# A unit of the rest's merge spread over three batches, and the gather ring grown at gather 460 in place of 450

## The chip, the cores and the metric

The kernel runs on one NeuronCore of a Trainium2 chip. The metric is the device time of one execution in microseconds (us), lower is better. A program is timed several times, and the median is compared.

## What is computed

The reference is one layer of a decoder for 512 prompt rows and 8 x 8 sample rows (576 rows in all, 1024 features, float32): an mLSTM branch and three groups of dilated window attention, merged by sigmoid gates, and after that a retrieval of experts. Only the last two parts matter here:

```python
merged = jax.nn.sigmoid(parts[14]) * branch_a + jax.nn.sigmoid(parts[15]) * branch_b
x = x + ga1 * _rmsnorm(merged @ prm['w_out'], prm['g_post1'])
h2 = _rmsnorm(x, prm['g_pre2']) * (1 + sc2) + sh2
# _peer: 8 heads, 16 experts of 16384 per row and head, chosen by two sets of 128 keys
act = gelu(jnp.einsum('td,thkd->thk', hb, u[eidx]))
out = jnp.einsum('thk,thkd->td', g * act, v[eidx])
```

`parts[14]`, `parts[15]` and the branches are products of the normalised input and of the branch outputs with weights. Each row takes 8 x 16 experts, and each expert is a row of 1024 numbers of `u` and 1024 of `v`, side by side in one table `uv` (8 KB a row).

## The kernel before, in words

**Tiles.** The 576 rows are four tiles of 128 (0 to 3) and one of 64 (tile 4, the samples, which takes two heads at once in its two halves). Everything up to the merge of tiles 0 and 1 ends before the stretch that matters; `output_and_experts` is that stretch. It starts the experts of tiles 0 and 1 as soon as these have been merged, and does the merge of the other 320 rows ("the rest") beside them.

**Blocks and batches.** A block `b` is a tile and a head: 16 blocks for tiles 0 and 1, 16 for tiles 2 and 3, 4 for tile 4, 36 in all. A block gathers 16 experts per row, so there are 576 gathers `n`, each of 128 table rows (1 MB). Two gathers are a batch `g` (8 to a block, `q` is the batch's place in its block, `g = 8 b + q`). What each engine does for a batch: GpSimd issues its two indirect DMAs (L1705) into a slot of `ring`; VectorE takes the dot product of the `u` half with the row's input (`dots_of`, L2040); ScalarE makes gelu, coefficient and a diagonal matrix of the coefficients (`diags`, L1887, L1892, L1896); TensorE multiplies the diagonal with the `v` half, two matmuls of 512 columns per gather (L1820), and adds up in PSUM.

**The ring.** The ring has 10 slots (`RING`). A gather `n` waits until the product of gather `n - 10` has been done (semaphore `s_v`), since that gives its slot back. From gather `GROWN` on there are 12 slots (`WIDE`): the two new ones lie in `trunk`, where the transposed inputs of the queries were. So gather `GROWN` waits for the last query product of all (`pool.wait_ge(s_q, query_count(ROUNDS, 0))`), and it and the next one wait for no product. `slot`, `in_front` and `arrivals` say which slot a gather has and which gather was there.

**Side work, in an order written out by hand.** All five engines walk through the same batches, and functions of `g` say what is done beside them. `query_piece`: TensorE's query products (L1720, 8 matmuls of 256 or 320 columns), in odd blocks at `q` 4 and 6, up to block 27. `scores` (L1733) at `q` 2. `route` on VectorE at `q` 6 (some 50 small instructions, which choose the experts of block `b + 2`), with an exponential on ScalarE. `side_merge(g)`: the rest's merge, 16 units `u` of three batches from `SIDE_FIRST` = 2 on. A unit is `rest_gate` (8 matmuls of 320 columns, L1760), `rest_sigmoid` on ScalarE two batches later (L1930), `rest_branch` (4 matmuls, L1769), and `rest_merged` on VectorE three batches after the branch (L2106, and L2109 in odd units). The two weight buffers `front.unit` are filled again by SP when the branch of the unit in them is done (L1656, L1658). Behind the units, from batch 50 on, come the 8 products with `w_out` (`rest_product`, L1782), one every two batches, of which the first waits for the last sum of `rest_merged`. In the rows these tiles have other names, since they lie in the same memory: `x` is the sigmoid's output, `h` the merged rest.

**The waits between the engines here.** `rest_gate(u)` waits for the sigmoid of unit `u - 1`, `rest_branch(u)` for the product of `rest_merged(u - 1)`, `rest_merged(u)` for `rest_branch(u)`, `rest_sigmoid(u)` for `rest_gate(u)`. Every engine works in order, so what an engine waits for holds up all its later batches.

## Time and profile before

| what | value |
|---|---|
| runs of the kernel (3) | 2593.35 us median, 2590.34 to 2606.07 |
| the profiled execution | 2573.82 us |
| its span, first to last instruction | 2572.0 us |
| mean granted TensorE clock | 0.92 |
| TensorE, VectorE, ScalarE, GpSimd busy | 85%, 48%, 29%, 28% of the span |
| moved by the DMA engines | 875.53 MB |

Times in the rows are from the span's start. The profile gives for each stretch the busy time of each engine, the TensorE clock granted (1.00 is full speed), the mean busy share of the 16 DMA engines and the GB/s that they moved.
### The profile page before, as it was taken

The page shows a single profiled execution, that of the slowest core. Times are in us where ns is not written, and L with a number is a line of the kernel's source. Part 1 is how long each engine was busy: PE and PEld are TensorE (multiplying, and loading weights), DVE is VectorE, ACT ScalarE, POOL GpSimd, SP SyncE. Part 2 cuts the span into 40 slices and gives each one's busy share as a digit, 9 for nine tenths or more (in the row PEclk, how much of TensorE's full clock was granted, in tenths as well). Part 3 has the DMA queues.
Part 4 walks back from the last instruction along what each step waited for, and adds up shares of the span by engine and source line. Part 5 has one row for each costly group of instructions (what it writes and reads, how often), then busy time and mean ns, then how long its engine had stood idle before and what let it go on. Part 6 is the DMA issues. An engine that isn't in the chain of part 4 may idle for free.

```text
span 2572.0 us, 25285 instructions
## 1 busy us (share of the span) xinstructions
PE 2185.7 (85%) x9074; PEld 1261.0 (49%) x9074; DVE 1228.4 (48%) x3177; ACT 757.9 (29%) x2195; POOL 732.5 (28%) x694
## 2 busy tenths in 40 slices
PE   6999989997687967999998877887879787878686
PEld 4777448865575834555554433343334333333221
DVE  1000001225332145666475686677676766566864
ACT  2000012332121024444433444343333333233422
POOL 0000001111101012444343434444434453344341
PEclk8999989997787988999999988988989898998899
DMA  8566649989772728999999999999999999799997
GB/s 345 221 251 251 226 147 320 310 303 354 257 278 106 270 98 318 391 411 395 388 412 361 407 411 373 415 417 416 414 414 411 419 410 410 306 420 420 420 420 302
DMA packets 146993, 875.53 MB, mean 340 GB/s; under 512 B 15944, under 2 KB 41832, under 8 KB 65076
## 3 DMA queue, kind: packets, MB, share of 16 engines
q0 software_dynamic: 85760, 691.32, 66.7%
q1 hardware_dynamic: 60156, 182.48, 19.2%
q8 instruction: 71, 1.16, 0.2%
q14 instruction: 54, 0.44, 0.0%
q10 hardware_dynamic: 952, 0.13, 0.0%
HBM read 861.53 MB, written 99.37 MB: 374 GB/s over the span
## 4 chain that ended last, share of the span: by engine, by line
PE 32%; DVE 14%; DMA 14%; issue 2%; ACT 2%; POOL 1%; ACTq 0%; POOLq 0%
PE ps L1820 22%; DMA pr_ring<-in_uv,pr_idx 12%; DVE pr_ring L2040 3%; PE ps L1720 3%; PE ps L1760 3%; PE ps L1769 1%; PE ps L1782 1%; PE ps L1742 1%; DMA x<-in_x_sample 1%; DVE pr_hot L2020 1%; DVE pr_hot L2024 1%; DMA pr_wq<-in_peer_wq 1%; DVE pr_ind L2001 1%; DVE pr_ind L1998 1%; DVE pr_pick L2027 1%
## 5 line engine op out<-in xcount | busy, mean ns | idle before, releaser
L1820 PE MATMUL ps<-pr_ring,pr_diag 128*128 128x512 f32 (+1 forms) x2216 | 1042.1, 624 | 231.5 <-ACT pr_diag L1896 231.5
L1705 POOL DMA_INDIRECT pr_ring<-in_uv,pr_idx x554 | 636.7, 1149 | 1043.9 <-PE ps L1820 843.4
L2040 DVE CUSTOM_DVE_ANT_0 pr_ring<-pr_ring,h 128x1024 f32<-128x1024 f32 x554 | 659.8, 1223 | 343.1 <-DMA pr_ring<-in_uv,pr_idx 341.6
L1820 PEld LDWEIGHTS ps<-pr_ring,pr_diag 128*128 128x128 f32 (+1 forms) x2216 | 423.2, 195 | 795.0 <-issue 468.2
L1887 ACT ACTIVATE pr_gel<-pr_dots 128x2 f32<-128x2 f32 x288 | 57.9, 201 | 534.9 <-DVE pr_dots L2040 534.1
L1896 ACT ACTIVATE pr_diag<-ident,pr_coef 128x128 f32<-128x128 f32 x512 | 173.5, 386 | 0.0
L1892 ACT ACTIVATE pr_coef<-pr_gel,pr_wgt 128x1 f32<-128x1 f32 x576 | 138.6, 287 | 27.3 <-ACT pr_gel L1887 0.8
L1720 PE MATMUL ps<-trunk,pr_wq 128*128 128x320 f32 (+2 forms) x544 | 134.0, 401 | 14.5 <-DMA pr_wq<-in_peer_wq 11.5
L455 PE MATMUL ps<-trunk,ap_ring 128*128 128x288 f32 x384 | 126.3, 411 | 2.9 <-PEq L182 2.9
L1720 PEld LDWEIGHTS ps<-trunk,pr_wq 128*128 128x128 f32 x544 | 101.6, 197 | 54.0 <-issue 14.4
L456 PE MATMUL ps<-trunk,ap_ring 128*128 128x288 f32 x384 | 125.2, 408 | 0.0
L369 DVE TENSOR_TENSOR late_rows<-ps,late_bias 128x512 f32<-128x512 f32 x2 | 1.4, 690 | 252.5 <-PE ps L359 252.5
L424 POOL DMA_DIRECT2D out_win_s<-in_cache x39 | 19.2, 493 | 339.7 <-PE ps L456 239.0
L668 DVE CUSTOM_DVE_ANT_0 pa_prob<-ps,pa_masks 128x256 f32<-128x256 f32 (+3 forms) x48 | 19.4, 454 | 186.2 <-PE ps L633 186.2
L459 PE MATMUL ps<-ap_ring,trunk 128*128 128x512 f32 (+1 forms) x240 | 104.5, 594 | 0.0
L837 PE MATMUL ps<-sa_ring,sa_spread 128*32 128x128 f32 x1664 | 70.0, 331 | 32.5 <-DMA sa_ring<-in_kcacheA 13.4
L455 PEld LDWEIGHTS ps<-trunk,ap_ring 128*128 128x128 f32 x384 | 72.9, 191 | 23.8 <-issue 4.2
L456 PEld LDWEIGHTS ps<-trunk,ap_ring 128*128 128x128 f32 x384 | 73.5, 192 | 20.5
L837 PEld LDWEIGHTS ps<-sa_ring,sa_spread 128*32 128x32 f32 x1664 | 57.1, 134 | 43.6 <-issue 16.5
L1887 ACT ACT_TABLE_LOAD x59 | 75.7, 1283 | 1.0
L1440 PE MATMUL ps<-trunk,h 128*128 128x256 f32 x256 | 60.2, 390 | 16.7 <-DMA h<-in_w_merge 16.6
L624 POOL DMA_DIRECT2D out_win_s<-in_cache x49 | 23.6, 487 | 178.1 <-PE ps L647 177.8
(315 smaller groups left out, 2268.2 us busy)
## 6 DMA issues: line engine op xcount, KB each, us to landing
out_win_s<-in_cache POOLq DMA_DIRECT2D x64, 1020.0 KB, 7.9
sa_ring<-in_cache SPq DMA_DIRECT2D x24, 1024.0 KB, 8.2
late_ring<-in_w_ada SPq DMA_DIRECT2D x8, 2048.0 KB, 17.8
sa_ring<-in_kcacheB SPq DMA_DIRECT2D x16, 1024.0 KB, 8.2
pr_wq<-in_peer_wq SPq DMA_DIRECT2D x16, 1024.0 KB, 18.8
out_win_s<-in_cache POOLq DMA_DIRECT2D x16, 1008.0 KB, 9.7
ap_ring<-in_w_attn_qk SPq DMA_DIRECT2D x6, 2048.0 KB, 21.0
h<-in_w_merge SPq DMA_DIRECT2D x16, 768.0 KB, 5.0
```

Source lines behind the costliest of these rows:

```text
L455: pe.matmul(ps[:, u % 2, 0:TH], wc, rhsT[:, c, 0:TH], **on)
L456: mm = pe.matmul(ps[:, 2 + u % 2, 0:TH], wc, rhsT[:, c, TH:T], **on)
L459: mm = pe.matmul(ps[0:r, u % 2, :], rhsT[:, c, tile_cols(j)], w[:, c, :], **on)
L837: mm = pe.matmul(o, self.spread[:, n % self.NZ, at:at + QT], self.ring[:, slot, (u * H + h) * P:(u * H + h + 1) * P], start=False, stop=la ...
L1705: pool.indirect_dma_start(row(n), None, d["uv"], bass.IndirectOffsetOnAxis(ap=idx[:, b % 4, j:j + 1], axis=0)).then_inc(arrived[slot(n)], 16)
L1720: mm = pe.matmul(ps[:, QUERY_BANK, 0:cols.stop - cols.start], e.wq[:, c, piece % 2 * P:(piece % 2 + 1) * P], e.h2T[:, c, cols], start=c == ...
L1760: mm = pe.matmul(ps[:, SIDE_BANK, 0:REST], front.unit[:, u % 2, c, :], k.hT[:, c, rest_cols], start=c == 0, stop=c == KD - 1)
L1820: mm = pe.matmul(ps[0:r, bank + half, :], diag[:, slot(n), 0:r], row(n)[:, o:o + CHUNK], start=h == 0 and j == 0, stop=b == FINAL[i] and j ...
L1887: act.activation(gel[:, o:o + BATCH], dots[:, o:o + BATCH], ACT.Gelu).then_inc(s_gel, 1)
L1892: act.activation(coef[:, o + j:o + j + 1], gel[:, o + j:o + j + 1], ACT.Copy, scale=wgt[:, b % 4, at:at + 1]).then_inc(s_cf, 1)
L1896: act.activation(diag[:, o + j, 0:r], k.ident[:] if i < PT else k.fold[:], ACT.Copy, scale=coef[:, o + j:o + j + 1]).then_inc(s_dg, 1)
L2040: ins = dve.tensor_tensor_reduce(u, u, e.h2[:, BLOCKS[b][0], :], 1.0, 0.0, ALU.mult, ALU.add, dots[:, slot(n):slot(n) + 1])
```

## The change

The unit's 8 gate matmuls are cut in two: 4 stand in the unit's first batch, 4 in its second, and the 4 of the branch move from the second to the third. What hangs on them moves along by one batch: the sigmoid (now two batches after the second half), `rest_merged` (three after the branch) and SP's load of the next weights (after the branch). The 8 products with `w_out` stay where they were. In the ring, `GROWN` is 460 in place of 450, so that the 10 gathers 450 to 459 still use the ring of 10, and the wait for the last query stands at gather 460.

```diff
--- before.py
+++ after.py
@@ -1528,7 +1528,7 @@
 def side_merge(g):
 
     u, step = divmod(g - SIDE_FIRST, 3)
-    return (u, step) if 0 <= u < 2 * KD and step < 2 else None
+    return (u, step) if 0 <= u < 2 * KD else None
 
 
 def side_product(g):
@@ -1552,7 +1552,7 @@
 
 
 WIDE = RING + 2
-GROWN = 45 * RING
+GROWN = 46 * RING
 
 
 def slot(n):
@@ -1649,7 +1649,7 @@
                         sp.wait_ge(s_q, query_count(piece[0] + 1, 0))
                         load_query_weights(sp, d, e, piece[0] + 1)
                     unit = side_merge(g)
-                    if unit and unit[1] == 1:
+                    if unit and unit[1] == 2:
                         u = unit[0] + 2
                         sp.wait_ge(s_branch, unit[0] + 1)
                         if u < 2 * KD:
@@ -1752,14 +1752,16 @@
                                           e.h2[0:r, i, c * P:(c + 1) * P], k.ident[0:r, 0:r])
                     mm.then_inc(s_tr, 1)
 
-                def rest_gate(u):
-                    pe.wait_ge(front.unit_ready[u % 2], 16 * (u // 2 + 1))
-                    if u >= 1:
-                        pe.wait_ge(s_sig, u)
-                    for c in range(KD):
+                def rest_gate(u, half):
+                    if half == 0:
+                        pe.wait_ge(front.unit_ready[u % 2], 16 * (u // 2 + 1))
+                        if u >= 1:
+                            pe.wait_ge(s_sig, u)
+                    for c in range(half * KD // 2, (half + 1) * KD // 2):
                         mm = pe.matmul(ps[:, SIDE_BANK, 0:REST], front.unit[:, u % 2, c, :], k.hT[:, c, rest_cols],
                                        start=c == 0, stop=c == KD - 1)
-                    mm.then_inc(s_gate, 1)
+                    if half:
+                        mm.then_inc(s_gate, 1)
 
                 def rest_branch(u):
                     if u >= 1:
@@ -1827,9 +1829,9 @@
                         if query_piece(g):
                             query(*query_piece(g))
                         unit = side_merge(g)
-                        if unit and unit[1] == 0:
-                            rest_gate(unit[0])
-                        if unit and unit[1] == 1:
+                        if unit and unit[1] < 2:
+                            rest_gate(*unit)
+                        if unit and unit[1] == 2:
                             rest_branch(unit[0])
                         if side_product(g) is not None:
                             rest_product(side_product(g))
@@ -1969,7 +1971,7 @@
                         if query_piece(g - 2):
                             query_taken(*query_piece(g - 2))
                         unit = side_merge(g - 2)
-                        if unit and unit[1] == 0:
+                        if unit and unit[1] == 1:
                             rest_sigmoid(unit[0])
                         if side_product(g - 2) is not None:
                             rest_copied(side_product(g - 2))
@@ -2133,7 +2135,7 @@
                                 finish(BLOCKS[b - 1][0])
                         g = b * PER + q
                         unit = side_merge(g - 3)
-                        if unit and unit[1] == 1:
+                        if unit and unit[1] == 2:
                             rest_merged(unit[0])
                         tile = side_tile(g)
                         if tile and tile[1] == 3:
```

On TensorE, at the first units (the batches 2 to 8; L1720 is a query, L1733 scores, L1820 the experts' products of a batch, L1760 the gate, L1769 the branch) there stood before:

```order
L1733 MATMUL ps<-pr_keysT,trunk 128x128 x2
L1760 MATMUL ps<-trunk,side_unit 128x320 x8
L1820 MATMUL ps<-pr_ring,pr_diag 128x512 x4
L1769 MATMUL ps<-trunk,side_unit 128x320 x4
L1820 MATMUL ps<-pr_ring,pr_diag 128x512 x8
L1760 MATMUL ps<-trunk,side_unit 128x320 x8
L1820 MATMUL ps<-pr_ring,pr_diag 128x512 x4
L1769 MATMUL ps<-trunk,side_unit 128x320 x4
```

and now (L1761 is the gate, L1771 the branch, L1822 the products):

```order
L1733 MATMUL ps<-pr_keysT,trunk 128x128 x2
L1761 MATMUL ps<-trunk,side_unit 128x320 x4
L1822 MATMUL ps<-pr_ring,pr_diag 128x512 x4
L1761 MATMUL ps<-trunk,side_unit 128x320 x4
L1822 MATMUL ps<-pr_ring,pr_diag 128x512 x4
L1771 MATMUL ps<-trunk,side_unit 128x320 x4
L1822 MATMUL ps<-pr_ring,pr_diag 128x512 x4
L1761 MATMUL ps<-trunk,side_unit 128x320 x4
```

Between any two batches' products stand four side matmuls now, where there were eight, four and none. On SP the loads around the last query weights of the merge (`pr_wq`) and the first weights of the `w_out` products (L1658) stood before:

```order
L1656 DMA side_unit<-in_w_merge 128x1536 [waits side_branch] x5
L1658 DMA side_unit<-in_w_out_b 128x1024 [waits side_branch]
L1525 DMA pr_wq<-in_peer_wq 128x8x256 [waits pr_query]
L1658 DMA side_unit<-in_w_out_b 128x1024 [waits side_branch]
L1663 DMA side_unit<-in_w_out_b 128x1024 [waits side_mm] x6
```

and now:

```order
L1656 DMA side_unit<-in_w_merge 128x1536 [waits side_branch] x5
L1525 DMA pr_wq<-in_peer_wq 128x8x256 [waits pr_query]
L1658 DMA side_unit<-in_w_out_b 128x1024 [waits side_branch] x2
L1663 DMA side_unit<-in_w_out_b 128x1024 [waits side_mm] x6
```

The first `w_out` weights have moved behind the load of the query weights. On GpSimd, the gathers around the growth (those into `trunk` are the two new slots; `pr_values` is the wait for a product, `pr_query` that for the last query) stood before:

```order
L1705 DMA pr_ring<-in_uv,pr_idx 128x2048 [waits pr_values,pr_routed]
L1705 DMA pr_ring<-in_uv,pr_idx 128x2048 [waits pr_values]
L1705 DMA trunk<-in_uv,pr_idx 128x2048 [waits pr_query]
L1705 DMA trunk<-in_uv,pr_idx 128x2048
L1705 DMA pr_ring<-in_uv,pr_idx 128x2048 [waits pr_values] x10
```

and now:

```order
L1705 DMA pr_ring<-in_uv,pr_idx 128x2048 [waits pr_values,pr_routed]
L1705 DMA pr_ring<-in_uv,pr_idx 128x2048 [waits pr_values] x11
L1705 DMA trunk<-in_uv,pr_idx 128x2048 [waits pr_query]
L1705 DMA trunk<-in_uv,pr_idx 128x2048
L1705 DMA pr_ring<-in_uv,pr_idx 128x2048 [waits pr_values] x2
```

The first row of each is gather 448. The wait for the query has moved ten gathers back.

## Rows read from the trace of the kernel before

**Rows 1.** The page's second part: GB/s in 40 slices of the span, 64.3 us each.
```profile
GB/s 345 221 251 251 226 147 320 310 303 354 257 278 106 270 98 318 391 411 395 388 412 361 407 411 373 415 417 416 414 414 411 419 410 410 306 420 420 420 420 302
```

**Rows 2.** Three stages: length, busy time (instructions) by engine, TensorE clock, DMA share, GB/s.
```profile
990.00:1401.00 411.00, 411.00 (x1254) 234.23 (x1252) 246.60 (x626) 169.10 (x462) 167.70 (x137) 1.00 0.98 388
...
2200.00:2250.00 50.00, 38.03 (x90) 18.27 (x90) 26.32 (x67) 13.97 (x49) 16.48 (x16) 0.90 0.67 273
2250.00:2550.00 300.00, 225.51 (x514) 82.05 (x513) 202.50 (x477) 99.95 (x339) 123.08 (x114) 0.91 1.01 420
```

**Rows 3.** Timeline of TensorE: the last branch, the first product with w_out, the end of the side work.
```profile
1275.59 4.47 PE L1760 MATMUL ps<-trunk,side_unit 128*128 128x320 f32 x16
...
1283.33 2.32 PE L1769 MATMUL ps<-trunk,side_unit 128*128 128x320 f32 x8
1285.48 7.03 PE L1820 MATMUL ps<-pr_ring,pr_diag 128*128 128x512 f32 x16
...
1292.79 4.47 PE L1782 MATMUL ps<-h,side_unit 128*128 128x320 f32 x16
...
1408.37 8.84 PE L1820 MATMUL ps<-pr_ring,pr_diag 128*128 128x512 f32 x16 [7.05 <-ACT pr_diag L1896]
```

**Rows 4.** Timeline of ScalarE: the last unit's sigmoid and the next diagonals.
```profile
1280.09 0.44 ACT L1930 ACTIVATE x<-ps 128x320 f32<-128x320 f32 x1 [4.81 <-PE ps L1760]
...
1282.53 0.68 ACT L1896 ACTIVATE pr_diag<-ident,pr_coef 128x128 f32<-128x128 f32 x2
```

**Rows 5.** Timeline of VectorE: the last unit's merge.
```profile
1285.75 0.49 DVE L2106 TENSOR_TENSOR x<-ps,x 128x320 f32<-128x320 f32 x1 [11.06 <-PE ps L1769]
```

**Rows 6.** Landing times: the 14 unit loads (L1656), then the query weights issued at 1272.
```profile
DMA to landing us min/median/max: 4.8/8.3/9.7
```
```profile
pr_wq<-in_peer_wq SPq DMA_DIRECT2D x1, 1024.0 KB, 14.0
```

**Rows 7.** Stretches of 10 us around the growth of the ring, columns as in rows 2.
```profile
2210.00:2220.00 10.00, 7.38 (x23) 3.99 (x21) 9.34 (x38) 4.42 (x11) 0.00 (x0) 1.00 0.82 341
2220.00:2230.00 10.00, 7.03 (x13) 3.42 (x14) 6.40 (x12) 2.53 (x10) 0.00 (x0) 0.66 0.02 7
2230.00:2240.00 10.00, 10.00 (x29) 5.01 (x27) 0.87 (x1) 1.65 (x7) 4.93 (x6) 1.00 0.48 173
```

**Rows 8.** Timeline of GpSimd: gathers 449 and 450.
```profile
2205.89 0.93 POOL L1705 DMA_INDIRECT pr_ring<-in_uv,pr_idx  x1 [0.30 <-issue]
2233.55 0.93 POOL L1705 DMA_INDIRECT trunk<-in_uv,pr_idx  x1 [26.72 <-PE ps L1720]
```

**Rows 9.** Timeline of TensorE in block 27: both query pieces, batch 222.
```profile
2209.48 4.47 PE L1720 MATMUL ps<-trunk,pr_wq 128*128 128x320 f32 x16
...
2222.97 6.00 PE L1820 MATMUL ps<-pr_ring,pr_diag 128*128 128x512 f32 x8 [5.59 <-ACT pr_diag L1896]
2228.80 4.47 PE L1720 MATMUL ps<-trunk,pr_wq 128*128 128x320 f32 x16
```

**Rows 10.** Timeline of VectorE: dot products of gathers 450 and 456.
```profile
2239.13 1.23 DVE L2040 CUSTOM_DVE_ANT_0 trunk<-trunk,h 128x1024 f32<-128x1024 f32 x1 [12.73 <-DMA trunk<-in_uv,pr_idx]
...
2254.47 1.23 DVE L2040 CUSTOM_DVE_ANT_0 pr_ring<-pr_ring,h 128x1024 f32<-128x1024 f32 x1 [1.24 <-DMA pr_ring<-in_uv,pr_idx]
```

**Rows 11.** Block 25, TensorE: the first query piece, and batch 206 behind the route.
```profile
2120.57 4.47 PE L1720 MATMUL ps<-trunk,pr_wq 128*128 128x320 f32 x16
...
2134.05 6.08 PE L1820 MATMUL ps<-pr_ring,pr_diag 128*128 128x512 f32 x8 [5.58 <-ACT pr_diag L1896]
```

**Rows 12.** Block 25, GpSimd: gathers 418 and 424.
```profile
2119.47 0.93 POOL L1705 DMA_INDIRECT pr_ring<-in_uv,pr_idx  x1 [0.30 <-issue]
...
2146.43 1.14 POOL L1705 DMA_INDIRECT pr_ring<-in_uv,pr_idx  x1 [5.09 <-PE ps L1820]
```

**Rows 13.** Block 25, VectorE: dot products of gathers 418 and 422.
```profile
2138.10 1.27 DVE L2040 CUSTOM_DVE_ANT_0 pr_ring<-pr_ring,h 128x1024 f32<-128x1024 f32 x1 [0.62 <-DMA pr_ring<-in_uv,pr_idx]
...
2148.03 1.23 DVE L2040 CUSTOM_DVE_ANT_0 pr_ring<-pr_ring,h 128x1024 f32<-128x1024 f32 x1 [1.26 <-DMA pr_ring<-in_uv,pr_idx]
```

**Rows 14.** Timeline of VectorE: the dot product of the last gather, 575.
```profile
2556.75 1.22 DVE L2040 CUSTOM_DVE_ANT_0 pr_ring<-pr_ring,h 128x1024 f32<-128x1024 f32 x1 [1.25 <-DMA pr_ring<-in_uv,pr_idx]
```

## The prediction

> **What bounds the kernel now.** I read the page's slices first. From slice 16 on (1029 us) the GB/s row stands near 410 to 420, with one deep dip, 306 in slice 34 (2186 to 2251 us) [rows 1]. So the experts' part is a stream of 576 gathers that mostly runs at what the DMA engines carry, and what counts there is time in which they carry nothing. Two stretches concern the change, and the table of stages tells them apart [rows 2].
>
> The first is 990 to 1401 us, where the side work stands. TensorE is busy for 411.00 of 411.00 us at clock 1.00, and the DMA engines at 0.98. The reader is to see that TensorE has no gap at all: its timeline goes from row to row with no bracket until 1401, where it catches up with its data and then waits 7.05 us for the next diagonals [rows 3]. This stretch is bound by TensorE's sum of work, and the DMA engines follow it.
>
> The second is 2200 to 2250, DMA share 0.67. From 2250 to 2550 it is 1.01 at 420 GB/s [rows 2], and the last gather's dot product starts at 2556.75 [rows 14], some 15 us before the end. So from 2250 on the end is set by when the stream of gathers resumed. In slices of 10 us the hole has shares 0.82, 0.02 and 0.48 [rows 7]. Against 1.01 that is 1.9 + 9.9 + 5.3 = 17.1 us of standstill. GpSimd's timeline says why: gather 449 is issued at 2205.89, gather 450 not before 2233.55, after 26.72 us of waiting for L1720, the query product [rows 8]. That query stands on TensorE behind batch 222, which itself waited for its diagonals while VectorE did the route, and ran 6.00 us at a lowered clock; the query starts at 2228.80 and takes 4.47 [rows 9].
>
> **The ring at 460.** The wait for the query goes from gather 450 to gather 460. Gather 450 then waits only for the product of 440, like any other. What does the stream do then? Block 25 does exactly the same things 16 batches earlier, without that wait: its first query piece starts at 2120.57, that of block 27 at 2209.48 [rows 9, 11], 88.91 us later, and batch 222 starts at 2222.97 where batch 206 (2134.05) plus 88.91 gives 2222.96. So I read the new block 27 from block 25, shifted by 88.91:
>
> - Gather 418, which has 450's place, was issued at 2119.47 [rows 12], and its dot product began at 2138.10, when it had landed [rows 13]. Shifted, 450 is issued at 2208.4 and lands at 2227.0, in place of 2239.13 [rows 10].
> - Landings follow each other by (2148.03 - 2138.10) / 4 = 2.48 us there [rows 13]. Gather 456 lands at 2227.0 + 6 x 2.49 = 2242.0, if it is issued in time.
> - It has to wait for product 446, which stands behind the second query piece. Gather 424, in its place, was issued at 2146.43 [rows 12], shifted 2235.3. That leaves 6.7 us. Gather 450 in the trace took 2239.13 - 2233.55 = 5.58 us on empty queues [rows 8, 10], so 456 is in time by 1.1 us. The engines' mean will still show a small hole: their standstill began at 2210 + 8.1 = 2218.1 (0.82 of ten at 1.01) and ended at 2240 - 4.8 = 2235.2, 1.7 after the issue [rows 7, 8]. Gathers 450 to 455 fill 6 x 2.49 = 14.9 us from 2218.1, to 2233.0, and 456 can't start before 2235.3 + 1.7 = 2237.0: 4.0 us. In block 25 the landings went on at their pace over the same place.
>
> Before, gather 456's dot product began at 2254.47 [rows 10]. The gain is 2254.47 - 2242.0 = 12.5 us. What is late next is TensorE's second query piece: it stops products 446 and later for 4.3 us, and it eats the other 4.6 of the 17.1. Bounds: the whole standstill, 17.1, if nothing of it comes back; 12.5 - 4.0 = 8.5 if the small hole delays landings too. I take 12.5, the value of the nearest rows.
>
> The ring of 10 for ten gathers more costs nothing by those rows: blocks 1 to 27 all ran on it. Gather 460 finds the query long done (it ends by 2233.3, and 460 comes at about 2241) and 461 needs no product either, so GpSimd is 12 ahead before the route of batch 230 begins.
>
> **The merge spread out.** Nothing is added or taken away: 16 units of 12 matmuls, before and after. A gate is 4.47 us with its tail, a branch 2.32, and two batches of products 7.03 [rows 3]. Start to start, a gate with the batch behind it is 1283.33 - 1275.59 = 7.74, a branch 1285.48 - 1283.33 = 2.15, two batches and scores 1292.79 - 1285.48 = 7.31. In a stretch in which TensorE never waits, the time is the sum of these, whatever their order. Smoother work lets GpSimd issue more evenly (the DMA engines were idle for about (1.01 - 0.98) x 411 = 12 us there), but a gather that lands sooner only waits longer for TensorE. At 1401 TensorE has done the same work at the same time. So the cost is 0, unless a wait appears. The candidates:
>
> - The sigmoid. It must be done, and the next diagonals made, before TensorE has done a batch and the branch behind the gate (3.44 + 2.15 = 5.6 us; 3.44 is half of the time for two batches without the scores). It starts at 1280.09, and the diagonals' instructions begin at 1282.53 and take 0.68 for two [rows 4]; the gate ended at 1280.06. That is 2.9 to 3.1 us, 2.5 to spare. The distance is the same after the change: the sigmoid follows the second half as it followed the whole.
> - `rest_merged`. VectorE waits 11.06 us for the branch [rows 5], and behind it wait the dot products of its batch. TensorE needs them three batches later, before and after. Only the first `w_out` product comes nearer: it waits for the last sum. Before, there were 7.31 us between branch and product; now there is one batch and the scores, 7.31 - 3.43 = 3.9 us. The two instructions of 0.49 take 1.0, so 2.9 are left.
> - The weights. A unit's load had five batches and now has four, about 20 us on TensorE; the 14 loads landed after 4.8 to 9.7 us [rows 6]. The first `w_out` load now stands behind the query weights on SP, which took 14.0 us from 1272.35 [rows 6], to 1286.4. Behind it, half a megabyte takes 1.3 us at 420 GB/s, and it is needed at 1292.79 [rows 3]. About 5 us are left.
>
> So the merge gives 0. Bounds: a gain of 8, if some of the idle 12 us could be turned into time after all; a loss of 6, if the first `w_out` product waits for both its weights and the sum by two or three us each.
>
> **The sum.** 2573.82 - 12.5 + 0 = 2561.3 for an execution like the profiled one (span 2559.5). The median of the runs shown is 2593.35, 19.5 above the profiled one; the same 12.5 off it gives 2580.9, which is 0.5%.
>
> **The rivals.**
>
> *The ring's gain does not come through.* Another wait might hold gather 450 or those behind it: VectorE's route holds up batch 222 for 5.59 us [rows 9], and a stream with 10 slots may drain there. Against it: block 25 has the same route, and in it the landings went on at 2.48 us [rows 13]. Time 2593.35, or 2590 with a remainder.
>
> *The merge gives too.* If TensorE's rows only look gapless and the real limit is how GpSimd gets slots back, four matmuls between batches in place of eight would free slots sooner. The idle 12 us of the DMA engines speak for it, 411.00 of 411.00 busy [rows 2] and the constant row lengths [rows 3] against it. It would give up to 8 more: 2573.
>
> *Slower: TensorE's clock falls in the merge.* Where TensorE has waited, the rows show a lower clock: behind the 7.05 us of idleness two batches took 8.84 us in place of 7.03 [rows 3], and batch 222 took 6.00 for one [rows 9]. If the more frequent changes between the groups opened small gaps, the clock could fall between 1001 and 1293 (292 us). In a stretch bound by TensorE each us at half speed costs half a us, so it decides from 25 us at the lower level on; a quarter of the stretch, 73 us, costs 36, less 12.5: 2617. Against it: clock 1.00 throughout, with as many changes of bank as there are products already [rows 2].
> The Trainium skill names this danger in "TensorE: Matmul & The Clock Gate", section "A second HAM failure mode: psum-queue depth-cycling": a kernel that goes round PSUM banks each iteration idles for moments between its groups, and its clock falls and rises again and again. By that rule the spread, with 16 more group changes, would be on the wrong side; the granted clock of 1.00 over the 411 us does not bear it out so far.
>
> **How the numbers follow.** The forecast 0.78 (2580.9, of its own 2575 to 2588); no gain from the ring 0.10 (2593); the merge gives too 0.09 (2573); slower 0.03 (2617). The range 2568 to 2593 takes in the bounds: 2593.35 - 17.1 - 8 = 2568, and 2593.35 - 8.5 + 6 = 2590.9, widened to the case without a gain. One per cent, about what a measurement of this kernel can tell from no change, is 25.9 us: 2567.4 to 2619.3. None of the cases reaches these bounds by itself; a median of few runs, which here spread over 15.7 us, may. Faster 0.06, within 0.91, slower 0.03.
>
> **What would show it.** In the new profile: no wait of GpSimd for the query product; gather 450 issued behind 449 by some 2.5 us; the DMA share of block 27 at 0.9 or more in each 50 us, with a hole of some 4 us just behind the second query piece; the last gather 12 to 13 us earlier. TensorE without a gap from 990 to 1401, clock 1.00, the end of the side work within a us of 1401. The forecast is wrong if TensorE reaches that point more than 3 us sooner or later, if the first `w_out` product shows a bracket, or if the hole in block 27 is more than 8 us.

## The result, and the profile after

Over 20 runs each, the changed kernel took 2572.26 us and the kernel before 2593.36; the ratio is 0.9947, with an interval of 0.9924 to 0.9970. By the ratio that is 0.53% or 13.7 us less (8 to 20), within 1%. The ratio is not the quotient of the two medians: that is 0.9919, or 21.1 us. The runs of one kernel spread over 33 us (the changed one) and 43 us (the one before), so I read the mechanism in the traces, by the *rest*: from the issue of the first gather to the end of the span. In the profiled execution of before the first gather is issued at 947.10, so the rest is 2572.0 - 947.1 = 1624.9 us. After the change it is issued at 968.07 and the span is 2581.1: 1613.0, which is 11.9 less. That the profiled execution after was longer than the one before (2582.94 against 2573.82) comes from the 21 us ahead of the first gather, in code that the change doesn't touch (last section). The functions have moved by two lines: products are L1822, gate, branch and `w_out` products L1761, L1771 and L1784.

The stages of the kernel after, moved by 21 us against [rows 2] (length, busy time by engine with instructions, TensorE clock, DMA share, GB/s):

```profile
1011.00:1422.00 411.00, 411.00 (x1255) 234.60 (x1253) 246.82 (x626) 168.88 (x462) 158.77 (x137) 1.00 0.98 388
2221.00:2271.00 50.00, 42.92 (x109) 20.94 (x108) 31.90 (x76) 16.17 (x58) 20.31 (x20) 0.93 0.96 382
```

The merge's stretch is the same in every column that counts: TensorE busy throughout, clock 1.00, DMA 0.98 at 388 GB/s. The stretch around the growth of the ring went from a DMA share of 0.67 to 0.96. Its 10-us windows answer to [rows 7]:

```profile
2230.00:2240.00 10.00, 7.90 (x25) 4.37 (x23) 9.31 (x41) 4.62 (x11) 2.84 (x3) 1.00 1.01 421
2240.00:2250.00 10.00, 6.50 (x8) 2.71 (x9) 9.07 (x15) 2.54 (x10) 1.33 (x1) 0.66 1.02 413
2250.00:2260.00 10.00, 10.00 (x31) 5.61 (x30) 4.93 (x9) 3.97 (x17) 2.91 (x4) 1.00 0.74 270
2260.00:2270.00 10.00, 10.00 (x28) 4.72 (x27) 3.93 (x8) 2.48 (x11) 7.60 (x8) 1.00 1.00 390
```

A hole of (1.01 - 0.74) x 10 = 2.7 us is left, where 17.1 were. GpSimd's timeline, against [rows 8] (gathers 449, 450, 456, and 460 and 461, the two that go to the new slots):

```profile
2226.41 0.94 POOL L1705 DMA_INDIRECT pr_ring<-in_uv,pr_idx  x1 [0.30 <-issue]
2228.71 0.94 POOL L1705 DMA_INDIRECT pr_ring<-in_uv,pr_idx  x1 [1.36 <-PE ps L1822]
...
2256.47 0.94 POOL L1705 DMA_INDIRECT pr_ring<-in_uv,pr_idx  x1 [5.08 <-PE ps L1822]
...
2262.87 1.32 POOL L1705 DMA_INDIRECT trunk<-in_uv,pr_idx  x1 [0.30 <-issue]
2264.49 0.94 POOL L1705 DMA_INDIRECT trunk<-in_uv,pr_idx  x1 [0.30 <-issue]
```

No wait names the query product L1720 any more. Gather 450 is 2.30 us behind 449 (27.66 before). Gather 456 waits for a product that stands behind the second query piece. When 460 and 461 are due, nothing holds them. TensorE there, against [rows 9]:

```profile
2229.99 4.47 PE L1720 MATMUL ps<-trunk,pr_wq 128*128 128x320 f32 x16
...
2243.50 6.68 PE L1822 MATMUL ps<-pr_ring,pr_diag 128*128 128x512 f32 x8 [5.60 <-ACT pr_diag L1898]
2250.01 4.47 PE L1720 MATMUL ps<-trunk,pr_wq 128*128 128x320 f32 x16
```

The first query piece gives the shift between the two executions at this point: 2229.99 - 2209.48 = 20.51 us. VectorE, against [rows 10] and [rows 14] (dot products of gathers 456, 457 and 575):

```profile
2262.14 1.23 DVE L2042 CUSTOM_DVE_ANT_0 pr_ring<-pr_ring,h 128x1024 f32<-128x1024 f32 x1 [1.90 <-DMA pr_ring<-in_uv,pr_idx]
...
2266.29 1.23 DVE L2042 CUSTOM_DVE_ANT_0 pr_ring<-pr_ring,h 128x1024 f32<-128x1024 f32 x1 [2.91 <-DMA pr_ring<-in_uv,pr_idx]
...
2565.87 1.23 DVE L2042 CUSTOM_DVE_ANT_0 pr_ring<-pr_ring,h 128x1024 f32<-128x1024 f32 x1 [1.25 <-DMA pr_ring<-in_uv,pr_idx]
```

With the shift taken off, gather 456 is dotted at 2241.63 and the last one at 2545.36, 12.8 and 11.4 us earlier than before. And the merge, TensorE against [rows 3] (last unit, first `w_out` product, end of the side work):

```profile
1296.57 2.32 PE L1761 MATMUL ps<-trunk,side_unit 128*128 128x320 f32 x8
1298.72 3.60 PE L1822 MATMUL ps<-pr_ring,pr_diag 128*128 128x512 f32 x8
1302.16 2.32 PE L1761 MATMUL ps<-trunk,side_unit 128*128 128x320 f32 x8
1304.31 3.60 PE L1822 MATMUL ps<-pr_ring,pr_diag 128*128 128x512 f32 x8
1307.74 2.32 PE L1771 MATMUL ps<-trunk,side_unit 128*128 128x320 f32 x8
1309.90 3.60 PE L1822 MATMUL ps<-pr_ring,pr_diag 128*128 128x512 f32 x8
1313.33 0.61 PE L1733 MATMUL ps<-pr_keysT,trunk 128*128 128x128 f32 x4
1313.77 4.47 PE L1784 MATMUL ps<-h,side_unit 128*128 128x320 f32 x16
...
1429.35 10.82 PE L1822 MATMUL ps<-pr_ring,pr_diag 128*128 128x512 f32 x19 [7.05 <-ACT pr_diag L1898]
```

Gate halves and branch take 2.15 us each from start to start, between batches of 3.43 (3.44 by others of the rows), and there is no bracket. From the first side product (1022.22) to where TensorE runs dry (1422.30) it is 400.08 us; before it was 400.35.

### The profile page after: what moved, and what is told of

It is laid out like the page before. It is cut to its first block, busy times and chain, and to the rows that moved or that the text cites. A ratio compares the mean times of both kernels' runs of the same rounds, so it can differ in the third digit from the quotient of the medians.

```text
span 2581.1 us, 25285 instructions
## 1 busy us (share of the span) xinstructions
PE 2206.7 (85%) x9074; PEld 1281.1 (50%) x9074; DVE 1229.0 (48%) x3177; ACT 757.5 (29%) x2195; POOL 729.9 (28%) x694
## 4 chain that ended last, share of the span: by engine, by line
PE 31%; DMA 15%; DVE 14%; issue 2%; ACT 2%; POOL 0%; ACTq 0%; POOLq 0%
PE ps L1822 21%; DMA pr_ring<-in_uv,pr_idx 12%; PE ps L1720 3%; DVE pr_ring L2042 3%; PE ps L1761 3%; PE ps L1771 1%; PE ps L1784 1%; PE ps L1742 1%; DMA x<-in_x_sample 1%; DVE pr_hot L2026 1%; DVE pr_hot L2022 1%; DMA pr_wq<-in_peer_wq 1%; DVE pr_ind L2003 1%; DVE pr_ind L2000 1%; DVE pr_pick L2029 1%
## 5 line engine op out<-in xcount | busy, mean ns | idle before, releaser
L1822 PE MATMUL ps<-pr_ring,pr_diag 128*128 128x512 f32 (+1 forms) x2224 | 1044.6, 623 | 211.2 <-ACT pr_diag L1898 209.5
L1822 PEld LDWEIGHTS ps<-pr_ring,pr_diag 128*128 128x128 f32 (+1 forms) x2224 | 424.3, 194 | 770.0 <-issue 472.3
L1720 PE MATMUL ps<-trunk,pr_wq 128*128 128x320 f32 (+2 forms) x544 | 134.8, 403 | 13.9 <-DMA pr_wq<-in_peer_wq 11.0
L1720 PEld LDWEIGHTS ps<-trunk,pr_wq 128*128 128x128 f32 x544 | 102.1, 198 | 53.6 <-issue 14.2
L837 PE MATMUL ps<-sa_ring,sa_spread 128*32 128x128 f32 x1664 | 75.2, 348 | 35.7 <-DMA sa_ring<-in_cache 14.9
L837 PEld LDWEIGHTS ps<-sa_ring,sa_spread 128*32 128x32 f32 x1664 | 60.7, 141 | 47.8 <-issue 17.2
L1761 PE MATMUL ps<-trunk,side_unit 128*128 128x320 f32 x256 | 74.1, 432 | 0.0
## 6 DMA issues: line engine op xcount, KB each, us to landing
ap_ring<-in_w_attn_qk SPq DMA_DIRECT2D x6, 2048.0 KB, 21.1
```

What stands on the lines that cost most here:

```text
L837: mm = pe.matmul(o, self.spread[:, n % self.NZ, at:at + QT], self.ring[:, slot, (u * H + h) * P:(u * H + h + 1) * P], start=False, stop=la ...
L1720: mm = pe.matmul(ps[:, QUERY_BANK, 0:cols.stop - cols.start], e.wq[:, c, piece % 2 * P:(piece % 2 + 1) * P], e.h2T[:, c, cols], start=c == ...
L1761: mm = pe.matmul(ps[:, SIDE_BANK, 0:REST], front.unit[:, u % 2, c, :], k.hT[:, c, rest_cols], start=c == 0, stop=c == KD - 1)
L1822: mm = pe.matmul(ps[0:r, bank + half, :], diag[:, slot(n), 0:r], row(n)[:, o:o + CHUNK], start=h == 0 and j == 0, stop=b == FINAL[i] and j ...
```

## The experiments

"Rest" is what it was above; "side" is the time on TensorE from the first side product to the end of the gapless stretch. The runs of a group were made on one chip, beside runs of the kernel before on the same chip, and the ratio is taken against those. Their medians differ from the 2593.36 of the table: 2589.87 for ring_only, spread_only, packed and never, 2584.93 for query5_450, query5, less_gate and late_pieces, 2583.10 for packed_2 and query5_2, 2582.86 for the last two. So medians of different groups are not to be compared. Each rest is that of one profiled execution. The two kernels that were profiled twice differed from themselves by 2.4 us (query5) and 5.9 us (packed), so differences of 3 us between rests are not told apart here, while the 12 us of the ring are.

| run | median, us | ratio (interval) | rest, us |
|---|---|---|---|
| before | 2593.36 | | 1624.9 |
| the change | 2572.26 | 0.9947 (0.9924 to 0.9970) | 1613.0 |
| ring_only | 2568.74 | 0.9948 (0.9916 to 0.9981) | 1610.0 |
| spread_only | 2593.15 | 1.0028 (1.0000 to 1.0056) | 1624.5 |
| packed | 2578.18 | 0.9957 (0.9927 to 0.9987) | 1621.1 |
| never | 2576.77 | 0.9946 (0.9920 to 0.9972) | 1612.1 |
| query5_450 | 2577.77 | 0.9945 (0.9916 to 0.9975) | 1611.8 |
| query5 | 2571.81 | 0.9938 (0.9910 to 0.9967) | 1610.3 |
| less_gate | 2562.18 | 0.9888 (0.9848 to 0.9928) | 1600.4 |
| late_pieces | 2565.57 | 0.9912 (0.9878 to 0.9945) | 1614.2 |
| packed_2 | 2579.09 | 0.9980 (0.9947 to 1.0012) | 1615.2 |
| query5_2 | 2570.82 | 0.9936 (0.9912 to 0.9961) | 1612.7 |
| x_first | 2569.28 | 0.9917 (0.9887 to 0.9947) | 1610.8 |
| query5_x_first | 2571.35 | 0.9967 (0.9938 to 0.9997) | 1609.6 |

**The two parts alone.** `ring_only` is the kernel before with the ring's step alone:

```diff
-GROWN = 45 * RING
+GROWN = 46 * RING
```

`spread_only` is the changed kernel with that line back, so it has the merge's step alone:

```diff
-GROWN = 46 * RING
+GROWN = 45 * RING
```

> The kernel before with GROWN at 460 and the merge as it was. I judge by the span from the first gather's issue to the end, since the part ahead of it differs by some 20 us between executions of unchanged code (1624.9 us before, 1613.0 after). My theory (the whole gain is the ring's): 1613, within 2 us, TensorE gapless from the first side product to the end of the side work in 400 us, gather 450 issued some 2.5 us behind 449. Rival (the spread merge carries part of the gain): 1616 to 1621. In time against the kernel before: -12 us by the first, -4 to -8 by the second.

> The changed kernel with GROWN back at 450: the merge spread alone. My theory: 1624.9 us from the first gather to the end, within 2 us, the hole of 17 us in block 27 back in full, TensorE's stretch of side work 400 us as before; time against the kernel before 0. Rival (the spread merge frees slots sooner and gives time): 1617 to 1621. Rival (it costs, by waits or by the clock): over 1628.

With the ring's step alone the rest is 1610.0, 3 us under the 1613 expected, and the side 400.35. With the merge's alone it is 1624.5, the side 400.09, and the hole is back:

```profile
2208.00:2258.00 50.00, 38.27 (x89) 18.36 (x90) 26.28 (x67) 13.32 (x46) 16.44 (x16) 0.90 0.69 281
```
```profile
2241.17 0.94 POOL L1705 DMA_INDIRECT trunk<-in_uv,pr_idx  x1 [27.07 <-PE ps L1720]
```

So the whole gain is the ring's. Time between two points confirms it: from the last query piece (1281.7 us behind the first gather before, 1281.9 after) to the scores of the block after the next (the second row of L1733 from there) it is 67.8 us before, 68.2 in spread_only, 54.9 in ring_only and 55.3 after the change. From the query piece to the end it is 343.2, 343.4, 331.0 and 331.1. What else differs between the rests lies ahead of the query piece (1279.0 us in ring_only, 1281.2 in spread_only).

**Packing the merge, twice.** If spreading does nothing, does the reverse? Gate and branch all go into the unit's first batch: twelve products, none, none (steps of the gate, of the branch, of the sigmoid, of `rest_merged` and of SP's load all `unit[1] == 0`).

> GROWN at 460, and the merge the other way: the 8 gate and the 4 branch matmuls of a unit all in its first batch, none in the other two. My theory (a stretch bound by TensorE's sum of work, whatever its order): 1613 us from the first gather to the end, within 2 us, TensorE gapless, side work 400 us, while the DMA engines' share in the stretch falls a little below 0.98. Rival (evenness matters, bursts of 6.5 us leave TensorE without data afterwards): brackets behind the bursts, 1 us or more in each of 16 units, 1625 or more.

> The kernel of the run called packed once more (ring grows at 460, gate and branch products of a unit all in its first batch). Its rest, from the issue of the first gather to the end of the span, was 1621.1 us against 1613.0 after the change and 1610.0 with the ring's step alone; two gaps in the stretch of side products gave 1.3 us of that, and some 6 us were lost at one place some 640 to 670 us behind the first gather, where no merge product runs. Theory: the 6 us belong to that execution and not to the kernel; the rest comes to 1612 to 1615 us, with the two gaps (1.0 to 2.0 us in all) back in the side stretch, and the ratio to 0.9940 to 0.9957. Rival: twelve products in one batch shift what follows so that a later stretch stalls; the rest comes to 1619 to 1623 us again, with the loss at the same place.

TensorE's timeline in the side work of `packed`, all its brackets there:

```profile
1049.73 7.13 PE L1820 MATMUL ps<-pr_ring,pr_diag 128*128 128x512 f32 x16 [0.45 <-ACT pr_diag L1896]
...
1237.44 3.70 PE L1820 MATMUL ps<-pr_ring,pr_diag 128*128 128x512 f32 x8 [0.81 <-ACT pr_diag L1896]
```

Twelve products in a row use the cover up twice, for 1.3 us in all, and in `packed_2` at the same two places for the same (0.46 and 0.81). That much the order of the merge can cost. Then `packed` took 62.5 us from one row of scores (615.5 us behind the first gather) to the next query product (678.0), ring_only 54.8 for the same stretch and `packed_2` 57.5. So the repeat was without most of that loss, and came to 1615.2, 0.2 over what its theory allowed. Its ratio, 0.9980, lies above the expected; the intervals of the two overlap, and I can't say more of it. What held packed up there is told below, with x_first.

**Never growing.** `GROWN = 58 * RING`: all gathers in ten slots.

> The changed kernel with a ring that never grows (10 slots to the end, no wait for the last query at all). My theory for the hole in block 27 (it was the wait alone): as in the changed kernel up to gather 460, and the stream goes on at 2.49 us a gather after the route of each block, as it did in block 25 with 10 slots: 1613 to 1616 us from the first gather. Rival (the 12 slots carry the later blocks, where VectorE has the finish of a tile beside the route): holes of 2 us or more in blocks 28 to 34, together 5 to 15, so 1618 to 1628.

The rest is 1612.1, less than 1 us from that of the change. So the two slots more bring nothing that shows in the last blocks either; the growth at 450 only cost.

**The query's second piece one batch earlier.** This attacks the wait from the other side: the piece stands behind batch 221 in place of 222, ahead of the route.

```diff
-    if b > 0 and b % 2 and q in (4, 6) and b // 2 + 2 < ROUNDS:
-        return b // 2 + 2, (q - 4) // 2
+    if b > 0 and b % 2 and q in (4, 5) and b // 2 + 2 < ROUNDS:
+        return b // 2 + 2, q - 4
```

(ScalarE takes it ahead of the route's exponentials.) `query5_450` has the ring grow at 450, `query5` and `query5_2` at 460.

> The changed kernel with GROWN back at 450, and the second query piece of each odd block behind batch 5 in place of batch 6 (on ScalarE its copy stands ahead of the route's exponential), so that it runs while TensorE waits for the diagonals behind the route. It doses the wait: the last query then ends some 11.5 us sooner (about 2221.7 in the times of the trace before, in place of 2233.3), gather 450 is still held, but for less. My theory (the hole is as long as gather 450 waits for that product): the hole in block 27 shrinks from 17 us to 5 to 6, from the first gather to the end 1613 to 1615. Rival (the hole comes from the 10 slots running dry behind the route, whatever the query does): hole unchanged, 1625.

> The changed kernel with the second query piece behind batch 5 (as in the run with 450). My theory of what is left of the hole (2.7 us against 1.01 in the changed kernel's profile: the second query piece holds up the product that gather 456 waits for): it goes to under 1 us, since the piece fills the 5.6 us in which TensorE waits for the route; 1611 us from the first gather to the end, within 2 us; TensorE's side stretch stays gapless at 400 us. Rival (TensorE waits at the earlier piece for ScalarE's copy of the first one): brackets on L1720, 1613 or more.

> The kernel of the run called query5 once more (the changed kernel with the second piece of each block's queries one batch earlier), beside the packed one on the same chip, to narrow its ratio, which was 0.9938 with an interval of 0.9910 to 0.9967. Theory: the hole of 2.7 us of the changed kernel is the only thing that it closes, so the rest comes to 1609 to 1612 us and the ratio to 0.9930 to 0.9945, 0.0005 to 0.0015 below the changed kernel's 0.9947. Rival: the hole is taken back by the drain at the end, and the ratio is 0.9947 or above.

GpSimd in `query5_450`, and the 10 us in which its hole lies:

```profile
2250.00 1.82 POOL L1705 DMA_INDIRECT trunk<-in_uv,pr_idx  x1 [15.13 <-PE ps L1720]
```
```profile
2247.00:2257.00 10.00, 8.70 (x25) 4.35 (x24) 7.88 (x16) 4.18 (x17) 5.78 (x5) 1.00 0.55 199
```

Gather 450 still waits for the query, but 15.13 us and not 26.72 [rows 8]. The hole is (1.01 - 0.55) x 10 = 4.6 us where 17.1 were, a little under the 5 to 6 expected, and the rest is 1611.8, better than the 1613 to 1615 that I expected. So the price of growing at 450 hung on where the query stood: with the query early, the rest is 13.1 us shorter than before even so. In `query5` no gather waits for a query piece, and the hole is gone:

```profile
2230.00:2240.00 10.00, 8.72 (x25) 4.49 (x25) 9.23 (x18) 4.18 (x17) 3.08 (x3) 1.00 1.02 423
2240.00:2250.00 10.00, 10.00 (x25) 4.48 (x24) 4.94 (x8) 2.54 (x10) 7.48 (x7) 1.00 1.01 416
2250.00:2260.00 10.00, 8.71 (x24) 3.86 (x23) 4.93 (x8) 2.80 (x11) 5.76 (x7) 1.00 1.01 421
```

The rest came to 1610.3 and, repeated, 1612.7, a little over what was expected of the second. Against the 1613.0 after the change that is within what two executions of one kernel differ by, so no gain from closing the small hole is shown.

**Is the side stretch bound by TensorE?** `less_gate` leaves out three of the four products of the gate's second half in each of the 16 units (48 matmuls; the gate is summed over five of its eight slices).

```diff
-                    for c in range(half * KD // 2, (half + 1) * KD // 2):
+                    for c in range(KD // 2) if half == 0 else (KD - 1,):
```

> The changed kernel with three of the four matmuls of the gate's second half left out (48 in all), so that the rest's gates are not the reference's: 48 x 0.54 = 26 us less for TensorE in its side stretch. My theory (the stretch is bound by TensorE's sum, and the DMA engines are idle for 8 to 12 us of it): the time falls by these 8 to 12 us and no more, then the stream of gathers is the bound, 1601 to 1605 from the first gather. Rival (TensorE only looks busy and the slots are what counts): under 4 us. Rival (TensorE bounds all the way to the end of the side work): 26 us, 1587.

A half of four products takes 2.15 us, so 48 take 48 x 0.54 = 25.9. The rest fell by 12.6, to 1600.4, and the side stretch from 400.08 to 386.12. TensorE's brackets say where most of the other half stayed, 8.9 us in all. Behind the longest one the clock was lower too, and a half gate took 4.60 us in place of 2.32:

```profile
1134.80 3.70 PE L1822 MATMUL ps<-pr_ring,pr_diag 128*128 128x512 f32 x8 [1.07 <-ACT pr_diag L1898]
...
1182.13 3.70 PE L1822 MATMUL ps<-pr_ring,pr_diag 128*128 128x512 f32 x8 [1.70 <-ACT pr_diag L1898]
...
1220.55 4.60 PE L1761 MATMUL ps<-trunk,side_unit 128*128 128x320 f32 x8 [6.12 <-DMA side_unit<-in_w_merge]
```
```profile
1016.00:1400.00 384.00, 375.11 (x1121) 211.61 (x1121) 240.87 (x594) 163.51 (x446) 147.28 (x129) 0.99 0.99 403
```

So TensorE's work does bound this stretch, but only for the first 13 us: then the gathers run at 403 GB/s with a share of 0.99, and diagonals and a unit's weights come late. In size that is the 12 us of idle DMA that the prediction read from a share of 0.98. The share itself rose by only 0.01, which is 4 us; it is the rate, 403 GB/s in place of 388, that fits the gain. Either way the time came by less work and not by another order.

**The wait at the head of the stretch.** Block 0's two query pieces both go behind batch 2, so that products come ahead of them (shown: TensorE's part; the scores of block 2, SP's load and ScalarE's copies move along).

```diff
-        return (1, q) if q in (0, 1) else None
+        return None
...
+                        if b == 0 and q == 2:
+                            query(1, 0)
+                            query(1, 1)
```

> The changed kernel with the two query pieces of block 0 both behind batch 2 (before: behind batches 0 and 1), the scores of block 2 behind batch 3. TensorE waits 11 us there for the query weights, with the products of batches 1 and 2 behind it in its order. My theory (everything from there to 1401 is TensorE's sum, so a wait at its head counts in full): the products of two batches, 6.9 us, move into the wait; the side stretch begins and ends 5 to 7 us sooner, 1606 to 1608 from the first gather. Rival (the stream of gathers can't follow, and TensorE waits for data further on): brackets between 1022 and 1422, and 1611 to 1613.

```profile
989.73 12.26 PE L1825 MATMUL ps<-pr_ring,pr_diag 128*128 128x512 f32 x24 [2.86 <-ACT pr_diag L1904]
1012.25 6.34 PE L1723 MATMUL ps<-trunk,pr_wq 128*128 128x256 f32 x16 [10.26 <-DMA pr_wq<-in_peer_wq]
```

Three batches run ahead of the query now, and TensorE waits 10.26 us for its weights all the same. After the change they were there at 1005.40; here they came 6.85 us later, though issued at nearly the same time (985.82 against 985.14). The side stretch began at 1022.63 against 1022.22, where 5 to 7 us sooner had been expected, and the rest is 1614.2 in place of 1606 to 1608: the theory failed. The ratio, 0.9912 from 5 runs, overlaps with the change's (up to 0.9945, from 0.9924), and shows no gain over it. A fit to the rows, not shown by a run of its own: the early products freed slots, gathers filled them, and these took the engines' time from the weights.

**What packed lost.** VectorE waits in each run for the rows of the last token tile, which SP issues right behind 1 MB of query weights. In `packed`:

```profile
1596.39 0.15 DVE L2077 RECIPROCAL op_rs<-op_rt 64x1 f32<-64x1 f32 x1 [18.13 <-DMA x<-in_x_sample]
```
```profile
1606.73 0.94 POOL L1705 DMA_INDIRECT pr_ring<-in_uv,pr_idx  x1 [18.45 <-PE ps L1820]
```
```profile
1600.00:1610.00 10.00, 7.32 (x11) 3.26 (x12) 9.59 (x34) 4.75 (x13) 1.55 (x2) 0.59 0.58 218
1610.00:1620.00 10.00, 5.48 (x10) 2.15 (x9) 9.04 (x24) 5.61 (x11) 2.34 (x3) 0.75 0.94 377
1620.00:1630.00 10.00, 10.00 (x22) 4.39 (x22) 9.55 (x16) 5.19 (x21) 6.11 (x4) 0.91 0.72 258
```

While VectorE waits, its dot products wait behind it, TensorE gets no diagonals and GpSimd no slots. The DMA engines stand still for 4.3 + 0.7 + 2.9 = 7.9 us behind it, about the 7.7 by which this stretch is longer than in ring_only. The wait was 12.22 us before, 13.56 after the change, 10.55 in ring_only, 9.37 in packed_2. `x_first` issues the rows first (shown: what moved; in `query5_x_first`, on top of query5, the weights go one batch later for it):

```diff
-                    piece = query_piece(g)
-                    if piece and piece[1] == 1 and piece[0] + 1 < ROUNDS:
-                        sp.wait_ge(s_q, query_count(piece[0] + 1, 0))
-                        load_query_weights(sp, d, e, piece[0] + 1)
...
                         sp.dma_start(e.x1[0:tile_rows(i), i, :], src).then_inc(front.s_xr[i - GROUP], 16)
+                    piece = query_piece(g)
...
```

> The changed kernel with one thing moved on SP: in the batch in which both are due, the 256 KB of the last token tile's rows (L1676) are issued ahead of the next 1 MB of query weights (L1525), not right behind them. In every run so far VectorE waited for these rows, for 9.3 to 18.1 us, with the longest wait in the run called packed, whose stream then lost 6 to 8 us. Theory: it is the 1 MB ahead in the queue that makes them late; they now land within 8 to 14 us of their issue, in place of 18 to 27, VectorE waits for them 0 to 4 us, and the rest from the first gather comes to 1609 to 1612 us (after the change 1613.0). Rival: what makes them late is the stream of gathers, which shares the engines; the landing stays at 16 us or more and the wait at 7 us or more, with the rest at 1611 to 1616.

> The run called query5 (the query's second piece one batch earlier) with the same order on SP: the last tile's rows ahead of the query weights, which are issued one batch later. Theory: both small losses go, the hole behind the second query piece and the wait for the rows; the rest comes to 1607 to 1610 us (query5 had 1610.3 and 1612.7) and the ratio to 0.9925 to 0.9940. Rival: the wait for the rows is made good by what follows, since the stream runs at its full rate before and after it; the rest stays at 1610 to 1613 and the ratio at 0.9936 or above.

```profile
1583.35 0.15 DVE L2079 RECIPROCAL op_rs<-op_rt 64x1 f32<-64x1 f32 x1
```
```profile
x<-in_x_sample SPq DMA_DIRECT2D x1, 256.0 KB, 7.5
```

The same rows landed in 7.5 us (7.4 in query5_x_first), where the kernel after the change took 22.2 and packed 26.9, and the bracket is gone: it was the place in the queue, not the gathers. What that is worth is another matter. From 1610 to 1630 the DMA share is 1.02 in x_first and 0.85 after the change, so a hole of 3.2 us is closed. But the row of scores that ends this part stands 746.4 us behind the first gather in x_first, 747.1 after the change, 746.2 in ring_only with its wait of 10.55, and 754.4 in packed. So a wait of 9 to 14 us is made good to within 1 us by what follows, which was the rival's reading; only the one of 18 us cost time. Why the rows took 26.9 us in that one execution of packed, and 18.0 in the other, is open. The rests are 1610.8 and 1609.6, inside what was expected and inside the spread of one kernel. The ratio of query5_x_first, 0.9967, missed the 0.9925 to 0.9940 expected and lies where the rival put it. The medians don't tell the versions apart: the ratios of x_first, 0.9917, and query5_x_first, 0.9967, contradict the order of their rests, and their intervals overlap. All versions but spread_only and packed_2 beat before by their intervals; that any kernel that does the whole work beats the change isn't shown by the times.

## Why the prediction was right

**The size and its cause.** Predicted were 2580.9 us, 12.5 below the median of before; measured 2572.26, inside 2568 to 2593, and by the ratio 13.7 below. The medians themselves fell by 21.1, so the median was missed by 8.6 us. The starting point was luck too: the median of 3 runs, 2593.35, came back as 2593.36 from 20, while the same kernel had 2582.86 to 2589.87 in the four later groups. The term is better judged by the trace: 11.9 on the rest, 12.5 between the two points around the growth.

**The ring at 460, term 12.5: right in mechanism and size, by a reading that was wrong in one place.** Gather 456 was to be dotted at 2242.0; with the shift off it came at 2241.63. The wait for L1720 is gone, 450 is issued 2.30 us behind 449 (some 2.5 expected), and what came late next is what was named, the second query piece. The small hole was put at 4.0 us and is 2.7. It did cost something, which the central value left out: gather 457 kept VectorE waiting 2.91 in place of the usual 1.25, and the last gather came 11.4 us earlier (12 to 13 expected). So taking 12.5 through to the end was too good by 1.1 us.

The wrong reading is that "in block 25 the landings went on at their pace over the same place". The pace of 2.48 was read up to gather 422, dotted at 2148.03 [rows 13]. The next two, in the trace of before:

```profile
2152.59 1.23 DVE L2040 CUSTOM_DVE_ANT_0 pr_ring<-pr_ring,h 128x1024 f32<-128x1024 f32 x1 [3.33 <-DMA pr_ring<-in_uv,pr_idx]
...
2157.14 1.23 DVE L2040 CUSTOM_DVE_ANT_0 pr_ring<-pr_ring,h 128x1024 f32<-128x1024 f32 x1 [3.31 <-DMA pr_ring<-in_uv,pr_idx]
```

Gather 424, in the place of 456, was 4.1 us behind that pace. Moved by 88.91 it gives 2246.05 and a gain of 8.4, not 12.5. Block 27 did better than its template because one thing differs, which the prediction did not list. In block 25 SP loads the next query weights and writes out two tiles just then, 1 MB and twice 0.5 MB; from 2180 to 2260 it issues nothing, since block 27 holds the last query:

```profile
2144.47 0.54 SPq L1525 DMA_DIRECT2D pr_wq<-in_peer_wq  x1
2145.06 1.66 SPq L1687 DMA_DIRECT2D out_y_p<-x  x2
```

At the 420 GB/s of [rows 2] those 2 MB are an estimated 5 us of the engines' time, enough for the 4.1. No run varied this, so it is read from rows and not shown. That the pace could be carried over the place was luck.

**The merge, term 0: right.** spread_only measured it: side 400.09 against 400.35, rest 1624.5 against 1624.9. Its ratio, 1.0028 (1.0000 to 1.0056), would by itself allow a loss of up to 14 us; that there is none is read from the trace. Two of the three distances came out as worked out, and the third had more room. The sigmoid's diagonals began at 1306.94 and took 0.68; TensorE needed them at 1309.90, so 2.3 us were left (2.5 predicted). `rest_merged`, shown below, ended at 1311.18, 2.6 us ahead of the first `w_out` product at 1313.77 (2.9 predicted), which has no bracket. Its weights, issued at 1293.33, had landed after 9.1 us, 11 us ahead of it (5 predicted).

```profile
1310.17 0.49 DVE L2108 TENSOR_TENSOR x<-ps,x 128x320 f32<-128x320 f32 x1 [9.40 <-PE ps L1771]
1310.69 0.49 DVE L2111 TENSOR_TENSOR h<-h,x 128x320 f32<-128x320 f32 x1
```

**The rivals.** "The ring's gain does not come through" falls with ring_only. "The merge gives too" falls with spread_only, and less_gate says why: the idle DMA time there can be had, but by work taken off TensorE; its order doesn't matter while it never waits. "The clock falls in the merge" falls with the 1.00 over the 411 us. So the failure that the Trainium skill describes in "TensorE: Matmul & The Clock Gate", "A second HAM failure mode: psum-queue depth-cycling", did not appear: with a change of group every 2.15 to 3.44 us the rows show no idle moment between groups.

The likeliest case had a chance of 0.78 and a range of its own, 2575 to 2588. That was narrower than a median of this kernel allows: the measured one lies below it, with the mechanism right.

One reading of [rows 1] was loose: from slice 16 on the row is not near 410 to 420 but for one dip. It is at 361 to 412 up to slice 24, and the 373 of that slice (1543 to 1607 us) is where the wait for the last tile's rows falls.

## What to carry to other kernels

A ring that changes its size at a point where the next slot is still held by other work makes the whole stream wait for that work; put the change where the holder is long done, or leave it out, since ten slots did as well to the end. A wait is not yet a price: 26.7 us of it cost 12, and 15.1 us no time that could be seen. Where an engine has no idle bracket over a long stretch, moving its work about is worth nothing as long as no wait appears (packing it cost 1.3 us), and taking work off it is worth something, until the next resource is full. In a queue that shares its engines with a saturated stream, a small load that is needed soon lands sooner ahead of the large one that isn't: here in 7.5 us in place of 22, though it moved the end of that part by less than 1 us. And a stretch taken as a template for another is to be read through to the place in question, on every queue.

## What was not expected

**The front of the kernel varies.** Unchanged code ahead of the first gather took 21 us longer in one profiled execution than in the other. Two stretches of the sample's attention, before the change and then after it:

```profile
650.00:700.00 50.00, 36.16 (x490) 29.29 (x491) 16.33 (x56) 10.09 (x25) 10.70 (x11) 0.75 0.64 230
700.00:750.00 50.00, 43.47 (x632) 36.50 (x631) 19.48 (x86) 14.39 (x35) 0.00 (x0) 0.86 0.84 304
```
```profile
650.00:700.00 50.00, 37.43 (x366) 30.20 (x358) 13.61 (x47) 6.39 (x16) 10.71 (x11) 0.54 0.51 183
700.00:750.00 50.00, 43.07 (x500) 38.52 (x503) 14.21 (x60) 12.47 (x29) 0.00 (x0) 0.67 0.70 250
```

TensorE is as busy in both, but at a granted clock of 0.54 and 0.67 in place of 0.75 and 0.86, and it gets through 866 records of matmuls in place of 1122. The 1664 records of L837 alone, from the first to the last, take 181.6 us before and 201.1 after, with a median of 273 and 360 ns: that is 19.5 of the 21 us. In the 20 runs of the changed kernel a lower mean clock mostly goes with a longer time, from 0.907 and 2588.32 us to 0.923 and 2560.43, though one at 0.917 took 2587.47. So executions differ, in a stretch that no edit touched and together with the clock granted there, by more than the whole change is worth. What makes the clock fall there wasn't tried.

**A late load hides in the average.** The wait of 9 to 18 us for 256 KB stood in every trace but the two with the rows first, the one of before as well, and I had not read it: it lay outside the stretches that the change touches. It fits what packed lost in that stretch, while taking it away hardly moved the time.
